# Attention values from the key side: value weights applied to the keys once per block, eight heads collected in one PSUM bank

## What is computed

```python
q  = (cq @ w_uq).reshape(B, L, 8, 128)            # 8 heads, latent width 128
kv = rmsnorm(c_kv, kv_norm_g)                     # 1024 tokens x 128
score = sum_h w[t,h] * relu(q_idx . k_idx)        # the indexer
sel = top_k(where(causal, score, -inf), 256)
logits = (q . kv[sel]) * 128**-0.5 + rel_bias
probs = softmax(where(valid, logits, -inf))
o = einsum("bthk,btkc->bthc", probs, kv[sel])     # 128 wide per head
o = einsum("bshc,hcd->bshd", o, w_uv)             # 128 -> 64 per head
y_attn = o.reshape(B, L, 512) * silu(g_attn)
```

## Time and profile before

| what | value |
| --- | --- |
| median of three runs | 3046.41 us (3042.95 to 3048.2) |
| profiled execution, first to last instruction | 3044.6 us |
| mean granted TensorE clock | 0.980 |
| busy: PE, DVE, ACT, POOL | 94%, 64%, 43%, 42% |
| attention of layer 0 (queries of block 0 to the transpose of block 7) | 480.8 to 684 us |
| attention of layer 1 | the same picture from 1147 to 1347 us |

### The profile page before, as it was taken

The page is one execution under the profiler, slowest core; times in us unless marked ns, Lnnn a source line. Parts: engine busy times, 40 slices in busy tenths (PEclk is TensorE's granted clock), DMA queues, the critical chain, the costliest instruction groups (busy, mean ns, idle before and its releaser), DMA issues.

```text
span 3044.6 us, 49166 instructions
## 1 busy us (share of the span) xinstructions
PE 2860.1 (94%) x19746; PEld 1749.1 (57%) x19746; DVE 1953.3 (64%) x3140; ACT 1323.3 (43%) x2341; POOL 1280.0 (42%) x1060
## 2 busy tenths in 40 slices
PE   7889998999979988999999999999999999999998
PEld 3438776874429667864466565664764444444443
DVE  3785997763589996644875665666663654444445
ACT  3353654652366646643344554454543322122222
POOL 1302482010602580012545846767661635555551
PEclk9999999999989999999999999999999999999999
DMA  8223241002201340021101111201122201111111
GB/s 292 110 70 122 84 154 52 12 22 104 94 14 43 125 139 29 12 87 59 67 29 42 70 42 42 70 31 66 43 85 110 70 28 56 56 56 44 54 44 74
DMA packets 50898, 213.45 MB, mean 70 GB/s; under 512 B 4680, under 2 KB 9968, under 8 KB 34032
## 3 DMA queue, kind: packets, MB, share of 16 engines
q1 hardware_dynamic: 42288, 195.63, 18.5%
q10 hardware_dynamic: 8384, 14.68, 1.4%
HBM read 190.36 MB, written 19.94 MB: 69 GB/s over the span
## 4 chain that ended last, share of the span: by engine, by line
PE 41%; DVE 3%; POOL 3%; ACT 2%; issue 1%; DMA 0%; ACTq 0%; POOLq 0%; DVEq 0%
PE big L284 7%; PE big L286 7%; PE big L285 7%; PE banks L284 4%; PE banks L286 4%; PE banks L285 4%; PE banks L1183 3%; POOL w_lo L596 2%; PE banks L1162 0%; PE banks L1153 0%; PE banks L1134 0%; PE banks L1164 0%; PE banks L1170 0%; DVE arena L2567 0%; DVE arena L2568 0%
## 5 line engine op out<-in xcount | busy, mean ns | idle before, releaser
L653 POOL TENSOR_TENSOR w_lo<-stage,w_hi 128x512 bf16<-128x512 f32 x340 | 429.7, 1295 | 367.3 <-ACT w_hi L1390 367.0
L646 POOL CAST w_hi<-stage 128x512 bf16<-128x512 f32 x252 | 179.6, 753 | 781.4 <-PE big L286 588.5
L284 PE MATMUL big<-w_hi,ht_hi 128*128 128x256 bf16 (+2 forms) x1280 | 358.0, 288 | 22.7 <-DVE arena L1913 4.7
L596 POOL TENSOR_TENSOR w_lo<-stage,w_hi 128x512 bf16<-128x512 f32 x174 | 249.6, 1445 | 263.6 <-ACT w_hi L1590 263.6
L285 PE MATMUL big<-w_lo,ht_hi 128*128 128x256 bf16 (+2 forms) x1280 | 357.9, 288 | 0.0
L286 PE MATMUL big<-w_hi,ht_lo 128*128 128x256 bf16 (+2 forms) x1280 | 357.8, 287 | 0.0
L284 PE MATMUL big<-ht_hi,w_hi 128*128 128x512 bf16 x816 | 310.2, 380 | 24.7 <-POOL w_lo L596 8.7
L286 PE MATMUL big<-ht_hi,w_lo 128*128 128x512 bf16 x816 | 310.0, 380 | 0.0
L285 PE MATMUL big<-ht_lo,w_hi 128*128 128x512 bf16 x816 | 309.8, 380 | 0.0
L284 PE MATMUL big<-arena,w_hi 128*128 128x512 bf16 (+1 forms) x716 | 222.5, 328 | 21.4 <-DVE arena L2154 8.4
L285 PE MATMUL big<-arena,w_hi 128*128 128x512 bf16 (+1 forms) x716 | 222.6, 328 | 0.0
(11 more groups left out here) (395 smaller groups left out, 7144.2 us busy)
## 6 DMA issues: line engine op xcount, KB each, us to landing
stage<-in_w SPq DMA_DIRECT2D x130, 1024.0 KB, 4.8
arena<-in_w_ada SPq DMA_DIRECT2D x48, 512.0 KB, 4.4
arena<-in_x SPq DMA_DIRECT2D x16, 512.0 KB, 9.2
xs<-arena SPq DMA_DIRECT2D x16, 512.0 KB, 2.6
arena<-xs SPq DMA_DIRECT2D x16, 512.0 KB, 7.2
gt<-arena ACTq DMA_DIRECT2D x16, 256.0 KB, 2.5
arena<-gt ACTq DMA_DIRECT2D x16, 256.0 KB, 2.6
out_x<-arena SPq DMA_DIRECT2D x8, 512.0 KB, 2.6
```

Source lines behind the costliest of these rows:

```text
L284: pe.matmul(out, ah, bh, start=start, stop=False, skip_group_check=onto)
L596: return pool.tensor_tensor(lo, x, hi, ALU.subtract)
L646: pool.tensor_copy(w_flat[0][:, w0 + c0:w0 + c1], stage[:, n % RAW_RING, c0:c1]).then_inc(s_w_hi_split, mark(s_w_hi_split, n, q))
L653: ins = pool.tensor_tensor(w_flat[1][:, w0 + c0:w0 + c1], stage[:, n % RAW_RING, c0:c1], w_flat[0][:, w0 + c0:w0 + c1], ALU.subtract)
```

## The change

The value weights are applied to the keys, not to the weighed keys: for each block s of 128 keys, PE makes V[s] = keys x value weights of all eight heads (3 matmuls of 512 columns), ACT and DVE split it into VAL. `weigh` then takes the transposed probabilities as the stationary operand and 64 columns of VAL as the moving one, and writes 64 columns of a PSUM bank that holds all eight heads of a block. Gone are the token-major keys (KVK), the operand OT with its two splits, the old `values`, and the copies to YR: the scaling reads the bank. The scaling moves from i-6 to i-4, `turn_y` from i-8 to i-6, and the last use of `uv` is marked inside the loop.

```diff
@@ indexer preparation: PE, ACT and DVE lose one step each
-                pe.wait_ge(s_latent_dve, when(s_latent_dve, "kv_n", l))
-                g = take(pe, "big", "kvtok", l)
-                for s in range(NT):
-                    ins = pe.transpose(g[:, s * P:(s + 1) * P], RAW[:, s * P:(s + 1) * P], ident)
-                ins.then_inc(s_gemm, mark(s_gemm, "kvtok", l))
...
@@ SP, reload of x for the residual
-                        sp.wait_ge(s_weigh, when(s_weigh, "uv", l, NT - 1, NH - 1))
+                        sp.wait_ge(s_weigh, when(s_weigh, "ov", l, NT - 1, NH - 1))
@@ PE
+                def values(s):
+                    g = take(pe, "big", "v", l, s)[:, 0:512]
+                    mm3(pe, g, [x[:, s * P:(s + 1) * P] for x in KVT], [x[:, 0, 0:512] for x in uv], True, True).then_inc(s_turn, mark(s_turn, "v", l, s))
+                def weigh(tb, h):
+                    if h == 0:
+                        pe.wait_ge(s_v_lo, when(s_v_lo, l, tb))
+                        take(pe, "o", "o", l, tb)
                     pe.wait_ge(s_pt_lo, when(s_pt_lo, l, tb, h))
+                    g = tile("o", "o", l, tb)[:, h * 64:(h + 1) * 64]
                     for s in range(tb + 1):
-                        ins = mm3(pe, g[:, 0:P], [x[:, s, :] for x in KVK], [x[:, s * P:(s + 1) * P] for x in PT[h % 2]],
-                                  s == 0, s == tb)
+                        ins = mm3(pe, g, [x[:, s * P:(s + 1) * P] for x in PT[h % 2]], [x[:, s, h * 64:(h + 1) * 64] for x in VAL], s == 0, s == tb)
...
                 queries(0)
-                for i in range(n + 8):
-                    if 8 <= i and steps[i - 8][1] == NH - 1:
-                        turn_y(steps[i - 8][0])
+                values(0)
+                for i in range(n + 6):
+                    if 6 <= i and steps[i - 6][1] == NH - 1:
+                        turn_y(steps[i - 6][0])
                     if i < n:
                         logits(*steps[i])
...
                     if 3 <= i < n + 3:
-                        weigh(*steps[i - 3], g)
-                    if 5 <= i < n + 5:
-                        values(*steps[i - 5], g)
+                        weigh(*steps[i - 3])
                     if 1 <= i <= n:
                         turn(*steps[i - 1])
-                chunk_used(l, "uv", s_weigh)
+                    if i < n and steps[i][1] == 5 and steps[i][0] < NT - 1:
+                        values(steps[i][0] + 1)
+                        if steps[i][0] == NT - 2:
+                            chunk_used(l, "uv", s_turn)
@@ ACT: the copies to YR and OT go, one copy per block comes
+                def values_high(s):
+                    act.wait_ge(s_turn, when(s_turn, "v", l, s))
+                    act.activation(VAL[0][:, s, :], tile("big", "v", l, s)[:, 0:512], ACT.Copy).then_inc(s_v_hi, mark(s_v_hi, l, s))
...
+                    if 1 <= i <= n and steps[i - 1][1] == 5 and steps[i - 1][0] < NT - 1:
+                        values_high(steps[i - 1][0] + 1)
                     if i < n:
                         tb, h = steps[i]
@@ DVE, in this order in an iteration
                         freed(s_lmax, "lg", l, tb, h)
+                    if 1 <= i <= n and steps[i - 1][1] == 5 and steps[i - 1][0] < NT - 1:
+                        values_low(steps[i - 1][0] + 1)
                     if 2 <= i < n + 2:
                         turned_lo(tb, h, 4 if tb >= 4 else 0)
-                    if 4 <= i < n + 4:
-                        tb, h = steps[i - 4]
-                        dve.wait_ge(s_ot_hi, when(s_ot_hi, l, tb, h))
-                        dve.tensor_tensor(OT[h % 2][1], tile("o", "o", l, i - 1)[:, 0:P], OT[h % 2][0], ALU.subtract).then_inc(s_ot_lo, mark(s_ot_lo, l, tb, h))
                     if i < n and steps[i][1] == 3 and steps[i][0] < NT - 1:
                         queries(steps[i][0] + 1)
-                    if 6 <= i < n + 6 and steps[i - 6][1] == NH - 1:
+                    if 4 <= i < n + 4 and steps[i - 4][1] == NH - 1:
                         step(dve.reciprocal(rin, s_(S_SUM8 + tb % 2 * 8, 8)))
+                        dve.wait_ge(s_weigh, when(s_weigh, "ov", l, tb, NH - 1))
+                        step(dve.tensor_tensor(YR[tb % 2].rearrange("p (h d) -> p h d", h=NH), tile("o", "o", l, tb).rearrange("p (h d) -> p h d", h=NH),
                                                rin.unsqueeze(2).broadcast_to((P, NH, 64)), ALU.mult))
...
                         dve.tensor_tensor(YR[tb % 2], YR[tb % 2], GR[tb % 2], ALU.mult).then_inc(s_ya, mark(s_ya, l, tb))
```

More of the change, by code:

```diff
@@ L186, in build @@
         s_xnew = ctx.enter_context(nc.semaphore("xnew"))
-        s_yr = ctx.enter_context(nc.semaphore("yr"))
+        s_v_hi = ctx.enter_context(nc.semaphore("v_hi"))
+        s_v_lo = ctx.enter_context(nc.semaphore("v_lo"))
         s_ya = ctx.enter_context(nc.semaphore("ya"))
@@ L339, in build @@
         KVT = [bf(at + 2048, 1024), bf(at + 2560, 1024)]
-        KVK = [bf(at + 3072, 1024).rearrange("p (s c) -> p s c", s=NT), bf(at + 3584, 1024).rearrange("p (s c) -> p s c", s=NT)]
+        VAL = [bf(4096 + 2048 * i, 4096).rearrange("p (s c) -> p s c", s=NT) for i in range(2)]
         KID = [bf(at + 4096, 1024), bf(at + 4608, 1024)]
@@ L1423, in _ @@
                 act.activation(KVT[0], RAW, ACT.Copy).then_inc(s_latent_act, mark(s_latent_act, "kvt_hi", l))
-                act.wait_ge(s_gemm, when(s_gemm, "kvtok", l))
-                act.activation(KVK[0], tile("big", "kvtok", l)[:, :].rearrange("p (s c) -> p s c", s=NT), ACT.Copy).then_inc(s_latent_act, mark(s_latent_act, "kvtok_hi", l))
                 act.wait_ge(s_latent_dve, when(s_latent_dve, "cq_lo", l, 1))
@@ L1517, in queries @@
                                    scale=-float(P) ** (-0.5)).then_inc(s_qt_hi, mark(s_qt_hi, l, tb))
+                def values_high(s):
+                    act.wait_ge(s_turn, when(s_turn, "v", l, s))
+                    act.activation(VAL[0][:, s, :], tile("big", "v", l, s)[:, 0:512], ACT.Copy).then_inc(s_v_hi, mark(s_v_hi, l, s))
                 queries(0)
-                for i in range(n + 8):
-                    if 8 <= i and steps[i - 8][1] == NH - 1:
-                        tb = steps[i - 8][0]
+                values_high(0)
+                for i in range(n + 6):
+                    if 6 <= i and steps[i - 6][1] == NH - 1:
+                        tb = steps[i - 6][0]
                         act.wait_ge(s_gemm, when(s_gemm, "yt", l, tb))
@@ L2069, in _ @@
                 dve.tensor_tensor(KVT[1], RAW, KVT[0], ALU.subtract).then_inc(s_latent_dve, mark(s_latent_dve, "kvt_lo", l))
-                dve.wait_ge(s_latent_act, when(s_latent_act, "kvtok_hi", l))
-                dve.tensor_tensor(KVK[1], tile("big", "kvtok", l)[:, :].rearrange("p (s c) -> p s c", s=NT), KVK[0], ALU.subtract).then_inc(s_latent_dve, mark(s_latent_dve, "kvtok_lo", l))
-                freed(s_latent_dve, "kvtok", l)
                 steps = [(tb, h) for tb in TBS for h in range(NH)]
@@ L2320, in turned_lo, with values_low @@
                     freed(s_pt_lo, "pt", l, tb, h, q0)
+                def values_low(s):
+                    dve.wait_ge(s_v_hi, when(s_v_hi, l, s))
+                    dve.tensor_tensor(VAL[1][:, s, :], tile("big", "v", l, s)[:, 0:512], VAL[0][:, s, :], ALU.subtract).then_inc(s_v_lo, mark(s_v_lo, l, s))
+                    freed(s_v_lo, "v", l, s)
                 queries(0)
-                for i in range(n + 8):
-                    if 8 <= i and steps[i - 8][1] == NH - 1:
-                        tb = steps[i - 8][0]
+                values_low(0)
+                for i in range(n + 6):
+                    if 6 <= i and steps[i - 6][1] == NH - 1:
+                        tb = steps[i - 6][0]
                         dve.wait_ge(s_ya_hi, when(s_ya_hi, l, tb))
```

35 lines of the change are left out of this document (6 added, 29 removed).

## The result

| | kernel before | kernel after |
| --- | --- | --- |
| median of the comparison | 3046.61 us (3042.95 to 3048.2) | 3057.45 us (3053.8 to 3062.89) |
| ratio, 95% interval | 1 | 1.0041 (1.0027 to 1.0056) |
| span of the profiled execution | 3044.6 us | 3056.9 us |
| PE busy | 94% | 92% |

The change made the kernel 0.4% slower: 10.8 us by the medians, 12.3 by the spans. The forecast was 3052 us, with a range of 3034 to 3064; the time lies at the upper end of the likeliest case's own range, 3046 to 3058.

A forecast was written before the change was run, and what follows sets the result against it. Rings across engines, not PE's sum, were taken to bound blocks 4 to 7 except query steps; PE set plain steps in 1 to 3. Per layer 7.8 - 3.1 - 1.7 = +3.0 us, +5.9 for two: 3052 us, range 3034 to 3064.

The forecast's parts named there:

- likeliest case: Whole kernel: the chain as summed, 3052 us with its own range of 3046 to 3058; chance 0.50.
- What bounds the kernel: Attention blocks 4 to 7: rings, not PE's sum, set the steps except query steps; `weigh` saving there worth 0.
- The move of the scaling: Query step, scaling now behind the queries' low part on DVE: +1.56 us in blocks 1 to 5, 1.1 to 1.2 in 6.
- relief: Scaling's old place at h = 5 in blocks 4 to 6: 0.4 us saved in each, 1.1 in all.
- rival of the harmless move: DVE's lateness at h = 4 is made good before PE needs it: 3036 us or some more; chance 0.16.
- V in the ring: V's matmuls and DVE low part in blocks 4, 5, 6: +0.55, +1.0, +1.25 us, in all +2.8.
- the ring: Loop in blocks 4 to 7 through logits, minimum and low part that frees the PSUM bank for `turn`; `weigh` stands beside it.
- Blocks 1 to 3: Hand-made chain after the minimum of h = 3: +1.4, +1.65 and +1.05 us, before PE savings of 0.3, 0.6 and 1.0.
- The products: `weigh` matmuls at 28 instead of 56 ns: -2.2 us a layer, in blocks 1 to 3 and block 4's first step.
- End of attention and indexer: Last `weigh` to `turn_y`: -3.1 us; indexer's second score step without kvtok: -1.7 us; both per layer.
- New weights keep the price: Rival: 64-column `weigh` products with new weights still take 56 ns: 3058 us; chance 0.02.
- The clock: Rival: PE idles before `turn_y` in blocks 1 and 2, the clock falls, 2.6 us each: 3062 us; chance 0.18.

The follow-up runs named there:

- run 4: Changed kernel with every `weigh` product in blocks 4 to 7 computed twice: 3048.71 us, ratio 1.0012.
- run 10: Kernel before with `weigh` cut to the product of the two high parts, a third of its matmuls: 3039.4 us, ratio 0.9979.
- run 1: Changed kernel with the scaling back at h = 5 and `turn_y` back at h = 7 of the next block: 3037.63 us, ratio 0.9968.
- run 6: Changed kernel without V for key blocks 5 to 7, whose products read V of block 4: 3046.08 us, ratio 1.0003.
- run 8: Changed kernel with the scaling ahead of the queries' low part and V in the spare "o" pool half, at other PE and DVE places: 3017.18 us, ratio 0.9904.
- run 3: Changed kernel with the transposes of keys to token-major and their splits put back, result unused: 3063.04 us, ratio 1.0055.
- run 7: Changed kernel with V alone moved to the spare "o" pool half and other PE and DVE places, scaling left: 3041.04 us, ratio 0.9983.
- run 9: Run 8's kernel with `turn_y` between `weigh` and `turn`, and both splits of its result one iteration later: 3024.62 us, ratio 0.9937.

## Why the prediction was right, and where it was not

**What bounds the kernel: right, shown.** "Something other than PE's sum sets the step" rested on one comparison in the earlier trace rows. Runs 4 and 10 show it from both sides: 17.5 us more in blocks 4 to 7 and 32 us less leave every plain step there as it was.

**The move of the scaling: right and shown at the query steps; the sum agrees partly by luck.** Forecast +1.56 each in blocks 1 to 5 and 1.1 to 1.2 in block 6, less 1.1 of relief: 7.8 a layer. The query steps grew by 1.56 in blocks 1 to 3, 1.57 in block 4, 1.38 in block 5 and 1.15 in block 6. Between run 1 and run 4, in both of which the clock held, the six blocks differ by 7.8 (layer 0) and 7.9 (layer 1). In block 5 the forecast was too high, since PE set that step before (5.53 us, 5.35 with less work in run 10). The relief was put too low. Run 1 and run 4 differ by 9.6 us in the query steps, where 8.9 was forecast, and by -1.8 us in all others, where -1.1 was; by blocks they differ by 0.84, 1.17 and 1.47 us in blocks 1 to 3, where the move was priced at 1.56, and by 1.77 in block 6, where it was 1.1 less 0.3. These misses cancel in the 7.8. The rival of the harmless move is refuted: DVE's lateness was not made good.

**V in the ring: right, shown.** 0.44, 1.02 and 1.25 us by run 6 against 0.55, 1.0 and 1.25.

**Blocks 1 to 3: right in sum, not taken apart.** The chain put down by hand for block 2 had the minima at 6.44, 8.88, some 10.6, 12.8 and 14.2 us behind that of h = 3; the trace of after has 6.44, 8.86, 10.57, 12.80 and 14.30. But it mixed the scaling, V and `turn_y`, so it did not say that V alone costs 1.1 to 1.2 us there. That is one part of why the expectation of run 8 was 10 us too high.

**The products: right in sum, not isolated.** The prediction put the blocks without the scaling's move at 7.8 - 7.8 = 0; run 1 has -0.2 and 0.0 there against before: the gain of block 3 pays for V. Block by block it is less close (+0.4, 0, -1.2, -0.2, +0.5 and +0.35 us for blocks 1 to 6 in layer 0): the forecast gain of some 0.5 us each in blocks 1 and 2 is missing, and the loss in blocks 5 and 6 is half or less of the forecast 1.0 and 0.95, in part because the query steps there became 0.2 and 0.6 us shorter. Nearly all that run 1 gains (8.2 us by the medians) comes from the two other terms, 2 x (2.9 + 1.6 to 1.8), some 9.

**End of attention and indexer: right.** -2.9 against -3.1; -1.56 to -1.84 at the place (run 3) against -1.7. The scaling at the end takes 0.69 us for each of its two large parts; before it was 0.95 for the one in the earlier trace rows, while POOL was busy for 3.20 us from 681.27, and POOL does nothing there now. "New weights keep the price" is refuted by the 29 ns.

**The clock: the step that failed.** The rival placed its fall ahead of `turn_y` in blocks 1 and 2 and priced it at 2.6 us a block. It came behind the query step of blocks 4, 5 and 6, at 0.6 to 1.0 us each. The prediction had asked where PE would be idle for long, and there it looked at short blocks alone, with 2.9 and 1.6 us of idle time; the trace has 2.53 and 1.97 us there, and the clock stayed at 1.00 in both profiles of the changed kernel. In runs 6 and 7 it did fall there in three cases of eight, so this part of the rival was possible; its price in block 2 was 1.3 us and not 2.6. In blocks 4, 5 and 6 the waits behind the query step were 2.12, 1.69 and 1.45 us, and it fell (in block 6 of layer 0 in one profile of two). In blocks 4 to 6 it had written that PE's `turn` waits for a bank that DVE frees behind the scaling, and used this for the ring, but did not carry it to PE's idle time. It also had the case as an alternative to the summed chain. Both were true at once: the chain's +7.8 was met by the six blocks wherever the clock held (run 4: 147.73 - 140.10 = 7.6 and 147.58 - 139.75 = 7.8), and the clock came on top.

**The sum.** Forecast +5.9 on the span, measured +12.3. Of the 6.4 us between, 4.2 are the clock in blocks 4 to 6 (run 4 against after). The other 2 are what is left when small terms of both signs are added: block 0 (+0.1 and +0.6), the stage between the layers (about +1), the tail (+0.6), the shorter saving at the end (+0.4), the start (-0.6). These are within what the same stretches differ between profiles, so they are not explained one by one.

## What to carry to other kernels

- An operation that is ready early belongs ahead of an instruction that will wait, not behind it: on one side of the queries' low part the scaling was free, on the other it cost 1.56 us a block, the clock fell in blocks 4 to 6, and the kernel was 20 us of 3057 slower. When a step is moved up, look for the engine's longest wait in the iteration it lands in, and on which side of it the step comes.
- Removing work from the busiest engine is worth only what the ring leaves: 17.5 us of PE's products a layer brought next to nothing in the long blocks, while the two placements decided the sign, from +0.4% to -1.0% with the same arithmetic.
- New work should take a buffer and a slot that no ring uses. V in the spare half of a pool, in DVE's waiting time, cost 6 us a layer less than in the ring's own tile (tile and places moved together).

## What the runs showed that I had not expected

- More matmuls made the kernel faster: doubled `weigh` in blocks 4 to 7 gave 3048.71 us against 3057 to 3059. With PE idle for 0.65 us instead of 1.69 ahead of `turn` in block 5, the granted clock stayed at 1.00 instead of 0.66 over the step. That accounts for 4.2 to 5.1 us; the rest of the gain is not explained.
- The length of a wait does not tell whether the clock falls behind it. In the changed kernel it held behind 2.53 and 1.97 us in blocks 1 and 2 and fell behind 2.12, 1.69 and 1.45 us in blocks 4 to 6. In run 7 it fell behind 1.97 us in layer 1 and held behind 1.97 us in layer 0.
- With identical code the clock fell or held at one place: block 6 of layer 0 had 1.00 in one profile of the changed kernel and 0.95 in the other, 1.0 us apart in length.
- Untouched blocks are reproducible to some 0.03 us (block 7: 29.09 to 29.12 in all runs but run 9), while the stretch ahead of attention ended between 478.3 and 486.6 us. A change worth 1 to 3 us is read at its place, not in the total.
